# Prompt attention's probabilities: dividing after the multiplication instead of before, with the splitting of h moved to an earlier stage

## The reference

```
def block(args):
    qn_b, qp_b, j = args
    s = (jnp.einsum('bqhe,bkhe->bhqk', qn_b, k_nope)
         + jnp.einsum('bqhr,bkr->bhqk', qp_b, k_pe)).astype(jnp.float32) * scale
    qpos = j * Q_BLOCK + jnp.arange(Q_BLOCK)
    s = jnp.where(kpos[None, :] <= qpos[:, None], s, -jnp.inf)
    p = jax.nn.softmax(s, axis=-1).astype(v.dtype)
    return jnp.einsum('bhqk,bkhv->bqhv', p, v)
```

## Time and profile before

| what | us |
|---|---|
| median of 3 executions | 2007.61 (2003.63, 2007.61, 2008.39) |
| the profiled execution's own time | 2004.98 |
| its span, first to last instruction | 2002.8 |
| PE busy in it | 1873.4 (94%) |
| DVE, ACT, POOL busy | 817.4, 596.1, 458.0 |
| mean granted TensorE clock | 0.969 of full speed |

### The profile page before, as it was taken

How to read it: one execution, slowest core, us unless ns; L and a number is a source line. 1 busy time by engine, 2 the same in 40 slices (tenths; PEclk the granted TensorE clock), 3 DMA queues, 4 the chain that set the end, 5 groups by cost and what they waited for, 6 DMA issues and landing times. The chain is left out here.

```text
span 2002.8 us, 31647 instructions
## 1 busy us (share of the span) xinstructions
PE 1873.4 (94%) x13519; PEld 1524.0 (76%) x13519; DVE 817.4 (41%) x1534; ACT 596.1 (30%) x1170; POOL 458.0 (23%) x363
## 2 busy tenths in 40 slices
PE   5998899988999887999989999999989999999998
PEld 3643455557999645666668899989889999999986
DVE  4016365675110243444540555555652115551433
ACT  3020334334111342322312343434342223232211
POOL 0000000000221105554304800000005544545300
PEclk8998999998999998999999999999989999999999
DMA  9002000001211326774312832222123335433322
GB/s 286 0 0 67 11 11 6 6 1 61 93 43 43 108 85 222 243 264 143 96 38 67 212 79 52 52 62 52 44 88 96 85 89 145 114 93 90 111 74 84
DMA packets 189734, 175.95 MB, mean 88 GB/s; under 512 B 47868, under 2 KB 155964, under 8 KB 189468
## 3 DMA queue, kind: packets, MB, share of 16 engines
q1 hardware_dynamic: 166444, 120.76, 20.6%
q0 software_dynamic: 20592, 52.63, 8.9%
q10 hardware_dynamic: 2560, 0.56, 0.2%
HBM read 153.73 MB, written 27.47 MB: 90 GB/s over the span
## 5 line engine op out<-in xcount | busy, mean ns | idle before, releaser
L625 DVE TENSOR_SCALAR sb<-sb 128x1024 int32<-128x1024 int32 (+4 forms) x145 | 101.2, 703 | 345.6 <-DMA sb<-in_w_in 149.2
L2745 POOL TENSOR_TENSOR weights_low<-sb 128x1536 fp32r<-128x1536 f32 x42 | 148.0, 3525 | 175.8 <-DVE sb L625 175.8
L2868 PE MATMUL ps<-h_high_again,weights_high 128*128 128x272 f32 x688 | 142.3, 288 | 2.0 <-ACT weights_high L2784 2.0
L2868 PE MATMUL ps<-h_high_again,weights_low 128*128 128x272 f32 x688 | 142.3, 288 | 0.0
L2868 PE MATMUL ps<-h_low,weights_high 128*128 128x272 f32 x688 | 142.3, 288 | 0.0
L2868 PEld LDWEIGHTS ps<-h_high_again,weights_high 128*128 128x128 f32 x688 | 108.3, 188 | 2.2 <-ACT weights_high L2784 2.2
L649 POOL TENSOR_TENSOR sb<-sb 32x1088 f32<-32x1088 f32 x8 | 19.8, 2479 | 387.4 <-ACT sb L660 387.4
L2868 PEld LDWEIGHTS ps<-h_high_again,weights_low 128*128 128x128 f32 x688 | 108.4, 188 | 0.0
L2868 PEld LDWEIGHTS ps<-h_low,weights_high 128*128 128x128 f32 x688 | 108.3, 188 | 0.0
L2214 PE MATMUL ps<-h_high_again,recurrence_weights_high 128*128 128x384 f32 (+1 forms) x432 | 105.9, 354 | 2.1 <-ACT sb L2030 1.2
L1075 POOL DMA_INDIRECT sb<-in_cache_kv_latent,sb x64 | 60.6, 948 | 163.0 <-PE ps L1285 74.6
(11 more groups left out here) (347 smaller groups left out, 4028.8 us busy)
## 6 DMA issues: line engine op xcount, KB each, us to landing
sb<-in_w_in SPq DMA_DIRECT2D x82, 512.0 KB, 4.1
sb<-in_w_branch SPq DMA_DIRECT2D x48, 256.0 KB, 4.6
sb<-in_x_prompt SPq DMA_DIRECT2D x16, 512.0 KB, 5.0
values_by_level<-values POOLq DMA_DIRECT2D x56, 128.0 KB, 4.5
sb<-values_by_level POOLq DMA_DIRECT2D x7, 896.0 KB, 7.7
out<-sb SPq DMA_DIRECT2D x10, 512.0 KB, 2.8
h_high_in_dram<-h_high SPq DMA_DIRECT2D x8, 544.0 KB, 6.9
h_high_again<-h_high_in_dram SPq DMA_DIRECT2D x8, 544.0 KB, 10.9
```

The costliest lines, as they stand in the source:

```text
L625: return nc.vector.tensor_scalar(high.bitcast(I32), x.bitcast(I32), -4096, None, ALU.bitwise_and)
L2745: nc.gpsimd.tensor_tensor(flat(wLowR[slot]), flat(wLow[slot]), flat(wHigh[slot]), ALU.subtract)\
L2868: mm = nc.tensor.matmul(bank(4 * (k % 2) + s, n=HS2), w[:, c, :], x[:, t0:t0 + HS2], start=c == 0 and part == 0, stop=c == DC - 1 and part ...
```

## The change

1. **Division.** `normalise` goes. In its place `invert(g)` takes the inverse of the row sum and multiplies the 128 x 128 identity by it, into one of three buffers `inverse`; it stands behind `high` in a step. `turn(g-1)` waits for `exp(g-1)` alone and turns unnormalised probabilities. `attend` has two more matmuls, 64 columns of ones times the two heads' diagonals, into the other half of its PSUM bank, which give every output row the inverses of its tokens; ACT copies them out (`keep_spread`, 128 x 128), and `out` multiplies instead of copying.
2. **Split of h.** The 8 masks, 8 subtractions and 8 roundings run during the latents' projection, through two staging buffers each; SP stores the 16 results of 544 KB to DRAM. In the prompt attention SP loads the low parts back at the block's start and the high parts when the last pair starts, and waits for them at the block's end. The eight stores in the gate block go.
3. **Gate weights' split** moves from steps 9 to 12 of the last pair to its steps 0 to 5 (two masks, four subtractions of half the width); ACT rounds in steps 4 and 7.
4. **Latents.** ACT squares the first two chunks right behind their evacuation, and the sums wait for five evacuated chunks instead of six. Nine turned tiles use four banks and four buffers; each is one copy of 288 columns, of DVE for even tiles and ACT for odd ones. The waits for the stores of latents and memory move from SP at the block's end to ACT before the values' copies in the next block.
5. **Values.** Their banks are 0, 2, 4, 6 instead of 0 to 3, and they wait no longer for the copies of the last units.
6. **Paged attention's start.** Half of the mask is loaded in the memory block, ahead of the cached keys. Groups 1 and 2 are collected once the requests' keys are turned (`s_kt`, which the last early turning step of that block signals). POOL's list in the paged block starts at group 3.
7. Some semaphores that nothing waits for are gone.

```
+                for c in range(DC):
+                    sp.wait_ge(s_hl, c + 1)
+                    sp.dma_start(lD[:, c, :], lowStageR[c % 2].bitcast(F32)).then_inc(s_hd[c % 2], 16)
+                    sp.wait_ge(s_hh, c + 1)
+                    sp.dma_start(hD[:, c, :], highStageR[c % 2].bitcast(F32)).then_inc(s_hd[c % 2], 16)
...
-                sp.wait_ge(s_st[0], 32 * 5)
-                sp.wait_ge(s_st[1], 32 * 4)
-                sp.wait_ge(s_mst, 32)
+                for i in range(2):
+                    sp.wait_ge(s_hd[i], 32 * DC // 2)
...
+                for c in range(DC):
+                    if c >= 2:
+                        dve.wait_ge(s_hd[c % 2], 32 * (c // 2))
+                    masked(highStage[c % 2], hT[:, c, :]).then_inc(s_hm, 1)
+                    dve.wait_ge(s_hm, c + 1)
+                    nc.vector.tensor_tensor(lowStageR[c % 2], hT[:, c, :], highStage[c % 2], ALU.subtract).then_inc(s_hl, 1)
...
-                            pe.wait_ge(s_c_ev, 6)
+                            pe.wait_ge(s_c_ev, 5 + k)
...
+                for c in range(DC):
+                    sp.dma_start(hLowR[c].bitcast(F32), lD[:, c, :]).then_inc(s_hr, 16)
...
+                sp.wait_ge(s_u, UNITS * HA)
+                sp.wait_ge(s_s, LAST_PAIR)
+                sp.wait_ge(s_qrot, HA)
+                for c in range(DC):
+                    sp.dma_start(hHighR[c].bitcast(F32), hD[:, c, :]).then_inc(s_hr, 16)
...
+                    if g % 2 and g >= 3:
+                        keep_spread((g - 3) // 2)
...
-                def normalise(g):
+                def invert(g):
                     dve.wait_ge(s_p, g + 1)
                     nc.vector.reciprocal(rinv[:, g % 32:g % 32 + 1], rsum[:, g % 32:g % 32 + 1]).then_inc(s_ri, 1)
                     dve.wait_ge(s_ri, g + 1)
-                    p = prob[g % 3][:, 0:128 * (tile_of(g) + 1)]
-                    nc.vector.tensor_scalar(p, p, rinv[:, g % 32:g % 32 + 1], None, ALU.mult).then_inc(s_pn, 1)
+                    if g >= 3:
+                        dve.wait_ge(s_sp, (g - 3) // 2 + 1)
+                    nc.vector.tensor_scalar(inverse[g % 3], ident, rinv[:, g % 32:g % 32 + 1], None, ALU.mult).then_inc(s_dg, 1)
...
-                    nc.vector.tensor_copy(oT[:, m, 128 * j:128 * j + 128], bank(6 + i % 2, n=128)).then_inc(s_oe, 1)
+                    dve.wait_ge(s_spe, i + 1)
+                    nc.vector.tensor_tensor(oT[:, m, 128 * j:128 * j + 128], bank(6 + i % 2, n=128),
+                                            spread[i % 2], ALU.mult).then_inc(s_oe, 1)
...
-                    pe.wait_ge(s_pn, g + 1)
+                    pe.wait_ge(s_p, g + 1)
...
+                    pe.wait_ge(s_dg, 2 * i + 2)
+                    for hh in range(2):
+                        mm = nc.tensor.matmul(bank(6 + i % 2, VA, 128, 128, VA * hh), ones[:, 0:VA], inverse[(2 * i + hh) % 3],
+                                              start=True, stop=True, skip_group_check=True)
+                    mm.then_inc(s_sp, 1)
...
-                wait_unit_out(pe, 1, U_K[-1])
-                wait_unit_out(pe, 1, U_QL)
...
-                pool.wait_ge(s_cs, NQ)
-                pool.wait_ge(s_co, HC)
+                pool.wait_ge(s_kt, UNITS)
                 gather(pool, 1)
+                gather(pool, 2)
```

More of the change, by code:

```diff
@@ L129, in build @@
         ident = keep.take(128)
+        ones_at = keep.at
         ones = keep.take(128)
@@ L309, in build @@
         krT = work.take(T)
-        natural = work.take(2, KVL + ROPE)
+        natural = work.take(4, KVL + ROPE)
         after_prob = after_attn_in + TILES * BW + 4 * 1024
@@ L381, in _, with high_part, square @@
                 act.dma_start(sinT[96:128, :], c_sin).then_inc(s_rot, 16)
+                def high_part(c):
+                    act.wait_ge(s_hl, c + 1)
+                    nc.scalar.copy(highStageR[c % 2], highStage[c % 2]).then_inc(s_hh, 1)
+                def square(n):
+                    x, c = (cqT, n) if n < 3 else (ckvT, n - 3)
+                    act.wait_ge(s_c_ev, n + 1)
+                    nc.scalar.activation(sq[n % 2], x[:, c, :], ACT.Square).then_inc(s_sqr, 1)
                 for n, (dst, _, _) in enumerate(chunk_dst):
+                    if n < DC // 2:
+                        high_part(2 * n)
+                        high_part(2 * n + 1)
                     act.wait_ge(s_c, n + 1)
@@ L387, in _ @@
                     ins.then_inc(s_c_ev, 1)
[L388 to L394, removed]
+                    if n < 2:
+                        square(n)
+                for n in range(2, 5):
+                    act.wait_ge(s_ssum, n - 1)
+                    square(n)
                 def memory(n):
@@ L403, in _ @@
                     memory(n)
+                for i in range(1, TILES, 2):
+                    act.wait_ge(s_nt, i + 1)
+                    if i >= 4:
+                        act.wait_ge(s_st[i % 4], 32 * (i // 4))
+                    nc.scalar.copy(natural[:, i % 4, :], bank(4 + i % 4, n=KVL + ROPE)).then_inc(s_nt_ev[1], 1)
             @block.vector
@@ L532, in build @@
         rinv = work.take(UNIT_STEPS // 2)
+        inverse = [work.take(128) for _ in range(2)] + [Arena(WORDS - 128, WORDS).take(128)]
         SCALE_A = float(QK) ** -0.5
@@ L552, in build @@
         s_ri = sem("row_sum_inverted")
-        s_pn = sem("probabilities_normalised")
+        s_dg = sem("inverse_on_diagonal")
+        s_sp = sem("inverse_spread")
+        s_spe = sem("inverse_spread_evacuated")
+        spread = [Arena(olat_at + 128 * i, olat_at + 256).take(128) for i in range(2)]
         s_pt = sem("probabilities_turned")
@@ L601, in build @@
         hHigh_at = work.at
-        hHigh = work.take(DC, T)
         hLowR = [rounded(f"h_low{c}", c * T, 1, T)[:, 0, :] for c in range(DC)]
@@ L807, in _ @@
                         high(g - 1)
+                        invert(g - 1)
                     if g % 2 and g >= 5:
@@ L1021, in build @@
         lat = [work.take(2, 4 * KVL) for _ in range(LSLOTS)]
+        lat = [lat[i] for i in (0, 2, 3, 1, 4, 5)]
         qpx = [work.take(2, 4, HS)]
@@ L1041, in build @@
         rinv5 = work.take(PAIRS)
-        maskNew = work.take(PAIRS, TN)
+        maskNew = [Arena(ones_at, ones_at + 2 * TN).take(2, TN), work.take(2, TN)]
         wv_all = work.take(2, HA, VA)
```

153 lines of the change are left out of this document (74 added, 79 removed).

## The result

Forecast 1976 us; measured **1972.33 us** (median of four, 1971.16 to 1974.55) against 2005.62 before (four runs, 2002.57 to 2008.39): a ratio of 0.9836, 95% interval 0.9816 to 0.9855. The profiled execution took 1971.16, its span 1969.3, 33.5 less than before; the mean granted clock is 0.981 instead of 0.969. PE's busy time falls from 1873.4 to 1861.3 us although the change adds matmuls, so part of the gain is fewer stretches at half clock.

A forecast was written before the change was run, and what follows sets the result against it. PE, busy 94% of the span, was taken as the bound. Terms −4.3 − 5.2 − 6.0 + 3.6 − 10 + 1.3 − 8.4 = −29.0 us, from 2004.98 to 1976; the forecast's own bounds are 1966 to 1984.

The forecast's parts named there:

- Sums of squares: Before the latents' turning: PE's 2.3 us wait goes and the half-clock stretch behind it gives back 2.0, sum −4.3 us.
- values: At the values: other banks remove a 2.7 us wait, and the half-clock stretch behind costs 3.3 less, sum −6.0 us.
- Rival C2: The half-clock stretches (2.0, 3.3, 1.4 us) stay, total 1983 us; chance 0.05.
- Latents: Latents' first turn to the next block: store waits go, SP's issuing is late next, 15.3 us becomes 10.0, sum −5.2.
- Division in three pairs: Pairs 1 to 3: wait moves from turn to scores, −0.8 a pair; small matmuls +2.0 a pair; sum +3.6 us.
- rival A: In the pairs the turn's wait leaves no heir at the scores: about 8 us more gain, 1968 us; chance 0.15.
- The last pair: Last pair of heads: first half −5, second half −7 from less DVE work, small matmuls +2, sum −10 us.
- Rival C: Gate weights' split and small matmuls hold the last pair as h's splits did, its −12 goes: 1988 us; chance 0.10.
- Memory block and paged start: Mask loads push cached keys back, +1.3 us; at the paged attention, barrier wait −7.0 and half clock −1.4, sum −8.4.
- Rival B: The pairs' clock falls through the moved gaps ahead of the scores, 9 us more, 1985 us; chance 0.10.
- Rival D: The eight reloads of h's high parts come back one after another, late at the block's end: 2011 us; chance 0.02.
- Rival E: All is given back elsewhere, a later block waiting for loads that were covered before: 2000 to 2010 us; chance 0.03.

The follow-up runs named there:

- experiment 4: Changed kernel with the odd latent tiles' stores issued by ACT and the even ones' by SP: 1965.84 us, ratio 0.9819 to the kernel before.
- 7: Changed kernel with inversion and output behind the next maximum, gate weights' split in idle time, mask loads later, latent stores in three groups: 1951.13 us, ratio 0.9746.
- experiment 3: Changed kernel with each gate weights' split in one piece behind maximum and exponential of the last pair's steps 3 and 5: 1964.78 us, ratio 0.9821.
- experiment 5: Changed kernel with the old load of h's split put back into the last pair's 16 steps as unused work: 1971.52 us, ratio 0.9853.
- experiment 9: Changed kernel with probabilities normalised ahead of the turn and the old load of h's split as dead work in the last pair: 1979.07 us, ratio 0.9887.
- experiment 1: Changed kernel with the division as before, probabilities normalised ahead of the turn and no small matmuls: 1960.75 us, ratio 0.9801.
- 8: Changed kernel normalising ahead of the turn, gate weights' pieces behind the normalisation, mask loads later, latent stores in three groups: 1955.78 us, ratio 0.9770.
- experiment 6: Changed kernel with group 1 collected after the last attention product again and group 2 behind the barrier: 1973.93 us, ratio 0.9859.

## Why the prediction was right, point by point

- **The total** was right within 4 us, and this is partly luck. In the profiled spans the gain is 4.5 us more than the sum's 29.0: some 12 that were not counted (5.7 in the three pairs, 5.3 behind the paged start, 0.6 at the values) stand against some 7 that did not come (3.0 at the memory block and paged start, 2.0 in the last pair, 1.2 at the latents, the rest in two small terms).
- **Sums of squares** (−3.9 for −4.3) and **values** (−6.6 for −6.0) were right, both the wait and the clock: the windows behind them are at 1.00. Rival C2 is refuted there. No run undoes either alone. The split of h now runs ahead of the sums; that stretch came out 0.4 us short of the forecast, so the split cost little there, as assumed.
- **Latents** (−4.0 for −5.2): the heir was named rightly, SP's issuing, and mis-sized: "a tile's two issues take 174.48 − 173.62 = 0.86 us" was taken from the first two tiles alone, and nine in a row took 0.96 each. Experiments 4 and 7 show issuing as the bound, with buffers next.
- **Division in three pairs** (−2.1 for +3.6). The mechanism was right: the wait moved to the scores, three or four per pair of 0.7 to 1.1 us, and rival A is refuted. In the third pair, which runs at 1.00 in both, the net is 61.83 − 60.95 = +0.9 for the predicted +1.2, though the small matmuls cost 8 x 0.32 = 2.6 for the 2.0. The sign is off since the ends of the first two pairs had stretches at 0.84 and 0.92 in the trace of before (280 to 301 and 343 to 363.5 us), which I had not read; after, they are at 1.00. That is why the first pair got 2.3 us shorter without rival A.
- **The last pair** (−8.0 for −10): here a step failed. "I leave 2.1 on the path" for the gate weights' split; it cost 5.2 (experiment 3), because each piece stands ahead of a maximum on the ring that the change made the bound, and half clock came with it. The first half took 27.2 for the predicted 24. The second half's −6.5 fits the −6 of the text, but the reasoning did not: 2.9 of it are busy time at a higher clock, which the sum did not name, as I took all of the 7.1 between the twin halves for DVE's work, though the last pair ran at 0.88 and 0.73. I also priced the four splits alone, and experiments 5 and 9 show that the splits and the division take the same wait away. Rival C was true for the first half, as far as the gate weights' split goes.
- **That the parts add** was an unstated step. I summed the division and the move of h's split as if independent. The table under experiment 9 shows that they do not add: of the last pair's 54.9 us, moving the splits alone takes 12.8, the division alone 3.1, and both together 8.8. With h's split moved, the division in the order of the change costs about 7 us over the four pairs (experiment 1); in the order of 7 and 8 it costs nothing in the last pair.
- **Memory block and paged start** together (−2.7 for −5.7): the barrier's wait fell by 7.1 as forecast, and PE's waits for cached keys grew by 1.1 of the forecast 1.3. What went missing is the stretch at 0.59 and a last attention product of 5.06 us for 3.67. Behind the start, −3.9 of −6.7 lie in the paged attention (260.9 to 257.0 us), whose first window is at 1.00, where I counted −1.4: the term came out near its larger bound of 4.2. As experiment 6 tells, that clock is not the rule in all variants.
- **The rest, −2.9**, is in the block of the recurrence, which the change does not touch. Without the block's first 20 and last 45 us, parts of which are below 1.00 in both traces, its windows of 20 us at 0.91 are three before and one after:

```profile
1193.24:1213.24 20.00, 20.00 (x204) 18.87 (x204) 10.43 (x23) 9.01 (x18) 0.00 (x0) 0.91 0.09 23
...
1342.88:1362.88 20.00, 20.00 (x182) 18.95 (x182) 11.53 (x23) 9.96 (x19) 0.00 (x0) 0.91 0.07 12
```

  The first is of the kernel before (with 1293 and 1373 us), the second the only one after. Such windows come and go between executions, and no cause was found.
- **Rival B** was refuted for three pairs: 1.00 with three or four waits of 1.06 and less in each. The argument against it was not sound: "the granted clock held 1.00 with 23.4 us of such waits in the block" was read from 300 to 330 us alone, and before the change the four pairs ran at 0.95, 0.97, 1.00 and 0.81. In the last pair the clock was below 1.00 after the change as well (0.91): behind the waits of 1.66 and 1.74 at the scores the attendings ran at half clock, behind that of 1.55 at full clock (1.53 us). The Trainium skill, "TensorE: Matmul & The Clock Gate", section "A second HAM failure mode: psum-queue depth-cycling", tells of a kernel in which frequent small idle times between groups of matmuls made the clock oscillate. The trace agrees only in part, since the waits of 1.06 and less left the clock at 1.00 and longer ones came with either.
- **Rival D** (late reload) was refuted: the gate block starts with a wait of 1.0 us, and in experiment 3 the stretch with the reloads is as short as its twin. **Rival E** (all given back later) is refuted too: no later block is longer by more than 0.7 us.

## What to carry to other kernels

When two edits remove work ahead of the same wait, price them together: one may be worth nothing, or less, beside the other, and a run with each undone alone tells which. When a wait moves instead of vanishing, list what stands ahead of the new wait on every engine's program order, and move everything that no one needs yet behind it; here that gave more than the division itself. An engine's idle time is a place for other work only at the point of its program where it idles, not one instruction later.

## What was not expected of the hardware

- Back to back, a store's issue on SP takes about 0.5 us from start to start whether it carries 128 KB or 16 KB of 128 rows, while one of 512 rows takes 0.77. So three groups in six issues (3.08 us for the four of 512 rows, 1.58 for the two behind them) save 4.2 us of the eighteen's 8.84, and not two thirds of it.
- Gaps of 1.06 us a step left TensorE's granted clock at 1.00 in three pairs of the changed kernel. Longer gaps in steps of the same kind came with half clock behind them in some steps (1.66 and 1.74 in the changed kernel) and at full clock in others (1.55 there, 1.66 in experiment 4, 2.86 in experiment 5), so the gap's length alone does not tell. Full stretches of untouched code fell to 0.91 in some executions and not in others; runs of one kernel differ by 10 us with mean clocks from 0.981 to 0.988.
